# Delta rule as a wave over the tiles, with output-projection halves between its last links

## What is computed

```python
kk = jnp.einsum('bnhtk,bnhsk->bnhts', k, k)
A = jnp.where(strict, beta[..., :, None] * kk * dec, 0.0)
M = A + jnp.eye(B_CHUNK)
W = lax.linalg.triangular_solve(M, rhs, left_side=True, lower=True, unit_diagonal=True)
W1, W2 = W[..., :B_DV], W[..., B_DV:]
qk = jnp.einsum('bnhtk,bnhsk->bnhts', q, k) * dec
def step(S, xs):                      # over the chunks
    u = w1 - jnp.einsum('bhck,bhkv->bhcv', w2, S)
    o = jnp.einsum('bhck,bhkv->bhcv', qd, S) + jnp.einsum('bhts,bhsv->bhtv', qkm, u)
    S = tot[..., None, None] * S + jnp.einsum('bhsk,bhsv->bhkv', kd, u)
    return S, o
# then, for each layer
mix = jnp.concatenate([oA, oB, oC, oD], axis=-1)
h = h + mix @ w['w_out'][i]
h = h + peer(rmsnorm(h, w['norm_ffn'][i]), ...)
```

## Time and profile before

| | |
|---|---|
| median of three runs | 3993.44 us (3984.37 to 3995.75) |
| profiled execution, its own time | 3997.22 us |
| its span | 3995.4 us |
| PE busy | 3868.2 us (97%) |
| DVE busy | 2860.9 us (72%) |
| POOL busy | 2291.2 us (57%) |
| ACT busy | 1533.9 us (38%) |
| mean granted TensorE clock | 0.979 |
| output projection (PE L1299), share of the chain that ended last | 3% |

### The profile page before, as it was taken

The page is one execution under the profiler, slowest core; times in us unless marked ns, Lnnn a source line. Parts: engine busy times, 40 slices in busy tenths (PEclk is TensorE's granted clock), DMA queues, the critical chain, the costliest instruction groups (busy, mean ns, idle before and its releaser), DMA issues.

```text
span 3995.4 us, 59452 instructions
## 1 busy us (share of the span) xinstructions
PE 3868.2 (97%) x23204; PEld 3453.5 (86%) x23204; DVE 2860.9 (72%) x4841; ACT 1533.9 (38%) x2349; POOL 2291.2 (57%) x1452
## 2 busy tenths in 40 slices
PE   8989999999999999999999999999999999999999
PEld 6778599999899999999577886999989999999993
DVE  5765369945888868888567552699458888788885
ACT  1443245553333333334314432555533333344343
POOL 0132078886777558888201310788867775587871
PEclk9989999999999999999999789999999999999999
DMA  4201146666899999999222011566668999999992
GB/s 122 52 13 60 53 173 213 213 219 216 304 320 319 328 350 365 380 380 368 95 64 41 13 70 48 175 213 210 225 210 301 331 319 332 346 384 387 389 348 71
DMA packets 417976, 900.99 MB, mean 226 GB/s; under 512 B 94497, under 2 KB 242209, under 8 KB 416033
## 3 DMA queue, kind: packets, MB, share of 16 engines
q1 hardware_dynamic: 272288, 552.91, 40.4%
q0 software_dynamic: 90112, 268.76, 18.7%
q10 hardware_dynamic: 55296, 75.52, 5.2%
HBM read 773.87 MB, written 123.15 MB: 225 GB/s over the span
## 4 chain that ended last, share of the span: by engine, by line
PE 52%; POOL 17%; DVE 13%; DMA 10%; issue 5%; ACT 2%; another core or an unknown queue 1%; DVEq 0%; SPq 0%; ACTq 0%; POOLq 0%
PE banks L1388 14%; POOL peer_gates L2103 8%; PE banks L839 7%; POOL u_stage L2119 6%; PE banks L1400 6%; DMA u_stage<-peer_ut 4%; PE banks L1462 4%; PE banks L1497 4%; PE banks L1299 3%; PE banks L1317 3%; DMA peer_gates<-peer_v,u_stage 3%; POOL u_stage L2111 2%; DVE normed L2762 2%; DMA gated<-dense_gelus 1%; PE banks L1443 1%
## 5 line engine op out<-in xcount | busy, mean ns | idle before, releaser
L2103 POOL DMA_INDIRECT peer_gates<-peer_v,u_stage x512 | 749.5, 1464 | 367.9 <-DVE normed L2762 166.2
L1462 PE MATMUL banks<-gated_parts,v_parts 128*128 128x320 f32 x6144 | 912.7, 310 | 25.6 <-DVE gated_parts L2809 20.9
L1462 PEld LDWEIGHTS banks<-gated_parts,v_parts 128*128 128x128 f32 x6144 | 904.0, 188 | 34.5 <-issue 34.2
L1388 PE MATMUL banks<-peer_x_parts,u_parts 128*128 128x448 f32 x3168 | 672.1, 369 | 8.2 <-issue 5.7
L1388 PEld LDWEIGHTS banks<-peer_x_parts,u_parts 128*128 128x128 f32 x3168 | 595.1, 190 | 58.2 <-issue 8.7
L2119 POOL DMA_INDIRECT u_stage<-dense_gelus,u_stage x256 | 390.4, 1525 | 106.7 <-issue 77.4
L1388 PE MATMUL banks<-peer_x_parts,low_s 128*128 128x448 f32 x1696 | 398.9, 367 | 1.7 <-issue 1.5
L2778 DVE SCALAR_TENSOR_TENSOR peer_gates<-peer_gates,u_stage 128x1024 f32<-128x1024 f32 x254 | 325.5, 1281 | 97.6 <-DMA peer_gates<-peer_v,u_stage 78.4
L2762 DVE SCALAR_TENSOR_TENSOR normed<-peer_gates,u_stage,normed 128x1024 f32<-128x1024 f32 x254 | 327.5, 1290 | 85.4 <-DMA peer_gates<-peer_v,u_stage 57.5
L1893 ACT ACTIVATE u_stage<-banks 128x448 f32<-128x448 f32 x256 | 138.8, 542 | 635.7 <-PE banks L1388 506.0
L2096 POOL TENSOR_TENSOR parts_a<-x,parts_a 128x1024 fp32r<-128x1024 f32 x64 | 169.8, 2675 | 361.0 <-ACT parts_a L1842 360.9
(11 more groups left out here) (359 smaller groups left out, 6595.8 us busy)
## 6 DMA issues: line engine op xcount, KB each, us to landing
v_stage<-peer_v SPq DMA_DIRECT2D x256, 512.0 KB
u_stage<-peer_ut SPq DMA_DIRECT2D x244, 512.0 KB, 5.2
dense_gelus<-u_stage ACTq DMA_DIRECT2D x256, 224.0 KB
gates<-peer_gates SPq DMA_DIRECT2D x16, 2560.0 KB
u_stage<-gates SPq DMA_DIRECT2D x64, 640.0 KB
gated<-dense_gelus SPq DMA_DIRECT2D x256, 160.0 KB
x<-peer_ut SPq DMA_DIRECT2D x64, 512.0 KB, 4.7
u_raw<-peer_ut SPq DMA_DIRECT2D x64, 512.0 KB, 5.0
```

The source lines that it names most:

```text
L1388: ins = mm(PS[:, d % 2, 0:DW], u_part(n, a, k), XR[:, b, k, DENSE0:TOK], start=(k == 0 and m == 0), stop=(k == KT - 1 and m == 2))
L1462: ins = mm(vc[k][:, 0:PW3], VR[:, s, b, k * 128:(k + 1) * 128], HR[:, s, a, :], start=(j == 0 and m == 0), stop=(j == NKEYS - 1 and m == 2))
L2103: eng.indirect_dma_start(out=GU[:, t % 4, :], out_offset=None, in_=din["peer_v"].rearrange("l i j d -> (l i j) d"), in_offset=bass.Indirec ...
```

## The change

The levels, the delta state and the output projection are no longer three stages in a row. They become one wave of steps 0 to 12: at step s, tile i is at level s - 3 - i, so that step 7, for example, holds the links (4,0), (3,1), (2,2), (1,3), (0,4). The turning and the products of the tiles (steps 0 to 6) run in the same steps. From step 10 the delta state of tile 0, 1, 2 follows (`corrected`, `delta_state`, `delta_out`), one tile a step, and the sample's delta rule. The projection's first half of tile 0 stands in step 12, the other halves between the last links behind it.

What goes with it: the sample's `head_sums` move from ahead of the state steps to step 0, those of the prompt tiles to steps 0 to 2. `sample_state` on DVE moves from step 4 to step 3, ahead of level 0. The masked matrix AM has two slots, in one place early and in another late, in place of three; POOL's first mask product waits for `hs_sample` and for the first mixer's last output; POOL's masks follow the scaled keys step by step. PI, UM, UT lie elsewhere, and the sample has its own UUS. The loads of `w_out` are issued when the sample's rows are turned and the prompt state is stored, ahead of the sample's delta state on SP. On DVE, `head_out` of the first mixer stands behind the third link of a step, `delta_head` behind all; ACT takes `rms` of tile 0 ahead of `squares(3)`, and DVE `wq_low(0)` behind two `scale`.

```diff
+    place["at"] -= 2 * 4 * 128
+    AM_LATE = region(2, 4, 128)
...
+    place["at"] -= NT * 2 * 128
+    AM_EARLY = region(2, 4, 128)
...
-    AM = region(RING, 4, 128)
...
+    HEAD_AT = {5: 0, 6: 1, 7: 2, 8: 3, 9: SAMPLE}
+    FIRST_LEVEL = 3
+    FIRST_STATE = FIRST_LEVEL + LEVELS[False]
+    LEVEL_STEPS = FIRST_STATE + SAMPLE
+    LEVELS_OF = [[(s - FIRST_LEVEL - i, i) for i in range(NT) if 0 <= s - FIRST_LEVEL - i < LEVELS[i == SAMPLE]]
+                 for s in range(LEVEL_STEPS)]
+    SUMS_AT = {0: (0, SAMPLE), 1: (1, 2), 2: (3,)}
+    STATE_ORDER = [0, 1, 2, SAMPLE, 3]
...
+            sp.wait_ge(pe_done, at("filled", "gt", L, SAMPLE, 1))
+            sp.wait_ge(sem("hs_p_stored"), at("hs_out", L))
+            for k in range(0, KT, 2):
+                sp.sent(f"wo{k}_loaded", eng.dma_start(WO[:, k:k + 2, :], din["w_out"][L, :, k:k + 2]).then_inc(sem(f"wo{k}_loaded"), 16), "wo", L, k)
             sp.wait_ge(dve_done, at("gs_sample", L))
...
-            sp.wait_ge(pe_done, at("levels", L))
```

PE's order of the steps:

```diff
+            for step in range(LEVEL_STEPS - 1):
+                state = step - FIRST_STATE
+                if step < NT:
+                    turned_rows(step)
+                if state >= 0:
+                    corrected(state)
+                if state == 0:
+                    decayed_keys(SAMPLE)
+                level(step, 0)
+                if 1 <= step <= NT:
+                    keys_turned(step - 1)
+                if state >= 0:
+                    delta_state(state)
+                if state == 0:
+                    sample_step(4)
+                level(step, 1)
+                if 2 <= step <= NT + 1:
+                    products(step - 2)
+                if state >= 0:
+                    delta_out(state)
+                level(step, 2)
+                for i in SUMS_AT.get(step, ()):
+                    head_sums(i)
+                if step == 2:
+                    state_step(SAMPLE)
+                if step in HEAD_AT:
+                    head_norm(L, HEAD_AT[step], "h", HSQ[:, HEAD_AT[step]])
+                level(step, 3)
+                level(step, 4)
+                level(step, 5)
+                if state == 2:
+                    projected(0, 0)
+                if 0 <= state + 1 < SAMPLE:
+                    decayed_keys(state + 1)
+                if state >= 0:
+                    head_norm(L, state, "g", GSQ)
+                if 1 <= state < 3:
+                    sample_step(4 + state)
+            projected(0, 1)
+            corrected(3)
+            projected(1, 0)
+            head_norm(L, SAMPLE, "g", GSQ)
+            delta_state(3)
+            projected(1, 1)
+            delta_out(3)
+            turn(3 * L + 1, 0)
+            projected(2, 0)
+            head_norm(L, 3, "g", GSQ)
+            projected(2, 1)
+            turn(3 * L + 1, 1)
+            for i in range(3, NT):
+                projected(i, 0)
+                projected(i, 1)
+                turn(3 * L + 1, i - 1)
```

`level(step, k)` issues `inverse_turned` and `level_left` of the step's k-th link, then `level_right` of the link before it. On POOL and DVE:

```diff
+            def level(l, i):
+
                 R, n = ROWS[i], LEVEL_AT[l, i]
+                if n == 0:
+                    pool.wait_ge(dve_done, at("hs_sample", L))
+                    pool.wait_ge(pe_done, at("filled", "ho", L, 3))
                 pool.wait_ge(dve_done, at("a", L, i))
-                if n >= RING:
-                    l0, i0 = LEVEL_SEQ[n - RING]
+                if n >= 2:
+                    l0, i0 = LEVEL_SEQ[n - 2]
                     pool.wait_ge(pe_done, at("filled", "pi", L, i0, l0))
                     if l0 == 0:
                         pool.wait_ge(dve_done, at("ti", L, i0, 1))
...
+            for step in range(LEVEL_STEPS):
+                if step + 1 < NT:
+                    log_rows(step + 1)
+                if step < NT:
+                    scaled(step)
+                for l, i in LEVELS_OF[step]:
+                    level(l, i)
...
+            for step in range(LEVEL_STEPS - 1):
+                state = step - FIRST_STATE
+                if step < NT:
+                    turned_rows(step)
+                if state >= 0:
+                    corrected(state)
+                    delta_state(state)
+                if step == FIRST_LEVEL:
+                    sample_state()
+                    dve.wait_ge(sem("hs_p_stored"), at("hs_out", L))
+                level(step, 0)
+                if 2 <= step <= NT + 1:
+                    products(step - 2)
+                level(step, 1)
+                level(step, 2)
+                if step in HEAD_AT:
+                    head_out(L, HEAD_AT[step], "h", HRT, HON, GA, par("hnorm"), 0)
+                level(step, 3)
+                level(step, 4)
+                if state >= 0:
+                    delta_head(state)
+                if 1 <= state < 3:
+                    sample_step(4 + state)
+            corrected(3)
+            for half in range(2):
+                add_h(L, 0, half, "wo", 3 * L + 1)
+            delta_head(SAMPLE)
+            delta_state(3)
```

More of the change, by code:

```diff
@@ L1248, in inner, with corrected @@
                        skip_group_check=True)
-            for i in range(SAMPLE):
-                decayed_keys(i)
-            inner(0)
-            for i in range(SAMPLE):
+            def corrected(i):
+                inner(i)
                 pe.wait_ge(act_done, at("drained", "w2", L, i))
@@ new lines, in _, with level @@
+            left_last = []
+            def level(step, k):
+                here = LEVELS_OF[step][k:k + 1]
+                for l, i in here:
+                    if l >= 2:
+                        inverse_turned(l, i)
+                    level_left(l, i)
+                for l, i in left_last:
+                    if l:
+                        level_right(l, i)
+                left_last[:] = here
+            for step in range(LEVEL_STEPS - 1):
[36 more added lines that the diff above has]
+                    sample_step(4 + state)
@@ L1845, in _ @@
             wq_high(1)
-            rms(3 * L + 1, 0)
             for i in range(1, NT):
@@ L2522, in products @@
                 dve.did(TT(DQ[0:R, i, :, 0:R], DQ[0:R, i, :, 0:R], b[0:R, :, 0:R], ALU.mult).then_inc(dve_done, 1), "drained", "kq", L, i)
-            for step in range(NT + 2):
-                if step < NT:
-                    turned_rows(step)
-                if step == 4:
-                    sample_state()
-                if step >= 2:
-                    products(step - 2)
-            dve.wait_ge(sem("hs_p_stored"), at("hs_out", L))
             def sample_step(l):
@@ L2551, in sample_step, with level @@
                     counts.same(("gs_sample", L), ("drained", "gs", L, i, 1))
-                    head_out(L, i, "g", GRT, GON, GB, par("gnorm").broadcast_to([128, 2]), 2)
-            for l in range(7):
-                for i in LEVEL_TILES[l]:
+            def level(step, k):
+                for l, i in LEVELS_OF[step][k:k + 1]:
                     R = ROWS[i]
@@ L2571, in _, with corrected, delta_state @@
                     counts.same(("xi", L, i, l + 1), ("drained", "dx", L, i, l))
[L2572 to L2577 removed]
+            def corrected(i):
                 dve.wait_ge(pe_done, at("filled", "ut", L, i))
[L2579 removed]
+                if i >= 2:
+                    dve.wait_ge(pe_done, at("filled", "go", L, i - 2))
                 b = bank("ut", L, i).rearrange("p (h v) -> p h v", h=8)
                 dve.did(eng.tensor_copy(UU[:, i % 2], b[:, 0:4]).then_inc(dve_done, 1), "drained", "ut", L, i)
+            def delta_state(i):
                 dve.wait_ge(pe_done, at("filled", "gs", L, i))
```

246 lines of the change are left out of this document (105 added, 141 removed).

## The result

The changed kernel is slower by a little: 4015.43 us (median of 20 runs, 3984.58 to 4028.44) against 3994.60 us (median of 20 runs of the kernel before, taken beside them). The ratio is 1.0041, with a 95% interval of 1.0023 to 1.0059. The forecast was +0.42%.

What follows compares the result with a forecast made beforehand. PE, by its work and clock, was taken to bound the stage. Waits +8.6 and clock +2 gave +10.6 us in layer 0, +6.5 in layer 1, together +17: 3993.4 becomes 4010 us, range 3998 to 4027.

Steps and rivals of the forecast that it cites:

- step 7: PE waits 3.7 us for POOL's mask of link (3,1), its slot held until DVE finishes head output 1.
- step 12: PE waits 3.8 us as corrected(2) on DVE stands behind delta_head(1) and sample_step(5).
- step 4: PE waits 2.4 us for POOL's mask of level 0, tile 1, queued behind scaled(4).
- step 3: PE waits 5.8 us for POOL's first mask, which waits for DVE's turning work and sample_state.
- clock term: Stage per layer: 35 us at half clock as now, but under wide work; 16 us lost against 14, 2 more.
- step 11: PE waits 1.3 us as corrected(1) on DVE stands behind delta_head(0).
- step 5: PE waits 1.3 us for a POOL mask slot that DVE frees only behind the products of tile 2.
- A: Rival: the clock holds behind the waits, 8 us less lost per layer; no change, 3994 us; chance 0.26.
- B: Rival: the wave covers its waits at POOL's two mask slots; faster, 3977 us; chance 0.16.
- C: Rival: the clock stays low from turning through the early levels, 15 us more per layer; 4040 us; chance 0.06.
- D: Rival: the projection's early halves wait for the weight loads; up to 9.4 us per layer; under 1 in 100.
- step 8: PE waits 2.9 us for POOL's mask, with the sample's level 0 behind head_out(2) on DVE.

Runs made afterwards that it cites:

- e1: Changed kernel with the first mixer's head outputs moved on DVE behind all links of a step; 3999.55 us (one run).
- e3: Changed kernel with delta_head(1) and sample_step(5) moved on DVE behind corrected(2), the copy of UU; 4009.02 us (one run).
- e2: Changed kernel with PE's first link (level 0, tile 0) moved behind keys_turned(2) and products(1); 3988.92 us (one run).
- e8: Changed kernel with head outputs, first link, delta_head(1)/sample_step(5), sample_state and POOL's masks all reordered; 3962.26 us (median of 10), ratio 0.9945 to the kernel before.
- e7: Changed kernel with the w_out loads made late again, waiting for the keys of tile 0; 4021.03 us (one run).
- e4: Changed kernel with four throwaway float32 products on PE ahead of the mask wait in links (3,1) and (4,1); 4011.39 us (one run).

## Why the prediction was right

The forecast was 4010 us with 3998 to 4027 as its own range, and 4015.43 was measured. It was right by its waits, and its clock term was sized too small in layer 0. A part is luck: in layer 0 the idle time of PE came out 1.8 us below the forecast and its work 4.8 above (6.8 against 2), and the two errors offset each other.

- **Waits.** Forecast by step: 5.8, 2.4, 1.3, 0.4, 3.7, 2.9, 1.3, 3.8, 2.1, in all 23.7 us. Measured: 5.5, 2.2, 0.8, 0.4, 3.6, 2.5, 1.1, 3.6, 2.1, in all 21.9. Each is where it was laid and, but for one, has the cause that was named, in both layers. e1 and e3 confirm the causes of steps 7, 8 and 12 by moving the queued work, e2 that of step 3 in part (it was cut, and `sample_state` was in the way of the bank as well). Those of steps 4, 5 and 6 are read from the order of the rows; e8 moves the work of step 4, but together with other moves. The idle time of PE grew by 6.8 us in layer 0 against 8.6.
- **The cause of step 11.** I had `corrected(1)` queued behind `delta_head(0)`. PE waits 1.1 us at that point, but for a bank: `head_out` (L2256) is the last reader of the bank of `go(0)`, which the next link wants. Same queue, another mark.

```profile
370.97 0.42 DVE L2256 TENSOR_TENSOR mixers<-banks,mixers 128x256 f32<-128x256 f32 x1
```

```profile
371.54 1.13 PE L1148 MATMUL banks<-mixers,x 128*128 128x128 f32 x8 [1.12 <-DVE mixers L2256]
```

- **The clock, mis-sized.** Forecast: 35 us at the lower clock per layer, 2 us of work more than before. The stretches show 0.90 and 0.91; with two levels, twice the shortfall times the length is 47 and 42 us; PE's busy time is 6.8 us longer in layer 0 and 1.3 shorter in layer 1 (where the forecast made it 2.1 shorter). My own bound for this term was 30 to 45, and layer 0 is just outside. The main part is steps 3 and 4: I allowed 10 us at the lower clock, but 269 to 292 has a clock of 0.63, which is 17 us, the two waits included. The products in between, with operands of 64 rows, took 4.21 us (L1120, above) where 2.37 is their time at full clock (the same group at 289.20). The other part is the projection: I had it as cover, not as a place that pays:

```profile
388.67 7.83 PE L1286 MATMUL banks<-mixers 128*128 128x512 f32 x16
...
405.28 9.75 PE L1286 MATMUL banks<-mixers 128*128 128x512 f32 x16
...
416.20 7.03 PE L1286 MATMUL banks<-mixers 128*128 128x512 f32 x16
```

The first half pays 0.8 us for the wait of step 12, the second 2.7 for the sample's narrow products ahead of it. This half took 8.4 to 9.8 us in both layers of every run that has it in this place, and 7.03 is the time of those behind it. So here the wide work put behind narrow work pays for the clock that the narrow work let fall.
- **The narrow sums** in their new place took 3.27 us, as in the last of the earlier trace rows, and not the 5.80 of the first. But the groups behind them pay: 1.87 in place of 1.06, as the fall that was forecast there.
- **The weights.** Nothing waits for them, and e7 confirms that their early loads bring nothing.
- **The rule on transposes.** The prediction held the trace against the Trainium skill, TensorE: Matmul & The Clock Gate, Part 4 (PE-mode transpose). In the stretch from step 5 on, where nearly every link begins with transposes, the clock was 0.94, and four transposes took 0.60 us, where four of the sixteen at half clock in the earlier trace rows took 0.92. So the trace disagrees with it here too: transposes run at full clock and don't keep it low among products. What a long stretch of transposes alone would do, no run shows.
- **The rivals.** A needed the clock to hold behind the waits of steps 7 and 8; the 2.07 us links show that it fell. B needed the wait of step 7 under 1 us; it was 3.6. With head outputs moved in DVE's list (e1) it became 0.9, and with all orders mended the kernel took the time that B would have had: e8 lies 0.55% under the kernel before, B 0.4%. B described a possible kernel, only not this one. C needed the clock low up to step 6; it was back by 287.78, still in step 4 (four transposes in 0.60 us). D, no.
- **The sum.** Layer 0 +13.6 against +10.6, layer 1 +6.9 against +6.5, together +20.5 against +17. The medians differ by 20.8 us, the ratio alone gives 16 (9 to 24 by its interval): the sum lies within. The profiled pair (+9.3) is lower, by the stretches outside the stages told of with the result. Two bounds were added up wrongly: all high ends of the waits give 10.3 us and not 11, and the bounds then give a range of 4002 to 4028 us, not 3998 to 4027. The measured time lies in both.

## What to carry to other kernels

When stages are folded into a wave, look beside the work at what stands ahead of each short, urgent instruction (a mask, a copy that frees a slot or a bank) in the in-order list of its engine: here moving a few calls within the lists of DVE, POOL and PE turned +0.41% into -0.55%. Price a wait on TensorE with the clock that it costs behind it: here about 1.5 us for the two short groups behind waits of 3.6 and 2.5 us, and 0.8 for a wide group. Narrow products cost clock too, up to 2.7 us in the wide group behind them. Before a filler is judged useless, see where the backlog that it should cover stands: the same halves were worth 1 to 3 us with the backlog ahead of them and 7.5 with it behind.

## What was not expected of the hardware

- The clock fell behind rather short waits: behind 2.52 us (step 8) the link took 2.07 and 1.61 us, the same as behind 3.63 us (step 7). Behind 1.12 us (step 11) it did not: 1.13 us. But the length of the wait doesn't decide by itself: behind 2.64 us in the kernel before (for L2542) and 2.23 us in e8 (for L1838) the next group took 1.13 and 1.16 us, in both layers.
- It returned fast or slowly. After step 7's wait, with 128-row products, the groups were back at 0.60 and 1.06 us by 318.71, 3.3 us on. After step 3's, with 64-row products among others and a short second wait, it was low from 273.50 to about 288, although PE was busy for 9 us of that without a gap. The 64 rows alone are not the reason: in layer 0 of e3 and of e4 the same list of work behind the same wait took the products of 64 rows from 4.21 to 2.90 and 2.98 us, and the group behind them ran at full clock (0.85 us in place of 1.49). What made the difference no run shows.
- The four operations of `sample_state` took 0.68 to 0.69 us each beside an idle POOL. Before, beside a busy POOL, the two that read no bank (L2459) took 1.28 and 1.43, and the two that read one (L2461) 0.69 as well: only the first kind grew longer.
